# First feed-forward of a three-part transformer kernel: 512-column products of both operand parts, padded operand rows, and constants loaded later

## The reference, cut to what matters

```
h = rms_norm(x, g)
gate, val = split(h @ w_up)              # 2816 columns each
conv = conv_b + sum over 3 taps of shifted gate * conv_w
x = x + rms_norm((gelu(conv) * val) @ w_down, g_post)
```

## Time and profile before

| | us |
|---|---|
| median of three runs (lowest, highest) | 890.5 (890.3, 890.86) |
| the profiled execution, whole | 892.5 |
| its span, from the first to the last instruction | 890.5 |
| mean granted clock of PE over the span | 0.998 |

### The profile page before, as it was taken

How to read it: one execution, slowest core, us unless ns; L and a number is a source line. 1 busy time by engine, 2 the same in 40 slices (tenths; PEclk the granted TensorE clock), 3 DMA queues, 4 the chain that set the end, 5 groups by cost and what they waited for, 6 DMA issues and landing times.

```text
span 890.5 us, 17166 instructions
## 1 busy us (share of the span) xinstructions
PE 877.2 (99%) x6192; PEld 805.6 (90%) x6192; DVE 669.5 (75%) x1098; ACT 545.4 (61%) x859; POOL 71.0 (8%) x65
## 2 busy tenths in 40 slices
PE   9999999999999999999999999999999899999997
PEld 8977999999999999999999999999899898888886
DVE  6976887777777966879866676799787787667666
ACT  7265744344344755978866666677497777666663
POOL 1000000000000043000000040200120000003102
PEclk9999999999999999999999999999999999999999
DMA  8963275555655555435656556444334365655641
GB/s 319 336 229 106 96 242 181 190 184 173 207 170 187 165 190 188 144 119 168 202 179 206 189 170 201 150 143 142 127 117 146 116 216 184 204 183 179 202 147 48
DMA packets 44293, 156.85 MB, mean 176 GB/s; under 512 B 5098, under 2 KB 5589, under 8 KB 44117
## 3 DMA queue, kind: packets, MB, share of 16 engines
q1 hardware_dynamic: 42889, 152.32, 51.8%
q10 hardware_dynamic: 908, 2.28, 0.8%
q0 software_dynamic: 448, 1.59, 0.5%
HBM read 155.11 MB, written 1.06 MB: 175 GB/s over the span
## 4 chain that ended last, share of the span: by engine, by line
PE 87%; DVE 6%; ACT 2%; DMA 2%; issue 1%; ACTq 0%; POOL 0%; DVEq 0%; POOLq 0%
PE ps L431 13%; PE ps L432 13%; PE ps L433 13%; PE ps L664 13%; PE ps L666 7%; PE ps L503 5%; PE ps L505 5%; PE ps L504 5%; DMA w_gate<-in_w_gate 2%; DVE w_lo L1526 2%; PE ps L439 1%; PE ps L480 1%; PE ps L474 1%; PE ps L473 1%; PE ps L939 1%
## 5 line engine op out<-in xcount | busy, mean ns | idle before, releaser
L1526 DVE TENSOR_TENSOR w_lo<-raw,w_hi 128x1024 fp32r<-128x1024 f32 x222 | 273.3, 1257 | 25.9 <-ACT w_hi L1112 23.4
L1112 ACT ACTIVATE w_hi<-raw 128x1024 fp32r<-128x1024 f32 x223 | 226.7, 1051 | 40.4 <-PE ps L505 18.3
L431 PE MATMUL ps<-op_hi,w_hi 128*128 128x256 f32 (+1 forms) x794 | 225.1, 284 | 0.4 <-DVE op_lo L1713 0.4
L433 PE MATMUL ps<-op_hi,w_lo 128*128 128x256 f32 (+1 forms) x794 | 223.6, 282 | 0.0
L432 PE MATMUL ps<-op_lo,w_hi 128*128 128x256 f32 (+1 forms) x794 | 223.6, 282 | 0.0
L431 PEld LDWEIGHTS ps<-op_hi,w_hi 128*128 128x128 f32 x794 | 149.9, 189 | 3.2 <-issue 1.8
L432 PEld LDWEIGHTS ps<-op_lo,w_hi 128*128 128x128 f32 x794 | 149.9, 189 | 1.1
L433 PEld LDWEIGHTS ps<-op_hi,w_lo 128*128 128x128 f32 x794 | 149.7, 189 | 0.0
L664 PE MATMUL ps<-mix,w_hi 128*128 128x512 f32 x384 | 136.3, 392 | 0.0
L666 PE MATMUL ps<-mix,w_lo 128*128 128x256 f32 x384 | 107.4, 280 | 0.0
L431 PE MATMUL ps<-mix,w_hi 128*128 128x256 f32 x336 | 95.8, 285 | 0.2 <-DVE mix L1883 0.2
(11 more groups left out here) (332 smaller groups left out, 1391.3 us busy)
## 6 DMA issues: line engine op xcount, KB each, us to landing
raw<-in_stream SPq DMA_DIRECT2D x283, 512.0 KB, 3.7
bias<-bias_rows POOLq DMA_DIRECT2D x1, 1024.0 KB, 12.7
work<-in_last_norm SPq DMA_DIRECT2D x1, 1024.0 KB, 5.7
result<-y SPq DMA_DIRECT2D x4, 256.0 KB, 2.0
x<-in_x SPq DMA_DIRECT2D x3, 256.0 KB, 5.2
y<-in_spans ACTq DMA_DIRECT2D x1, 640.0 KB
raw<-in_stream SPq DMA_DIRECT2D x2, 256.0 KB, 3.2
bias<-bias_rows POOLq DMA_DIRECT2D x1, 512.0 KB, 15.7
```

The source lines that it names most:

```text
L431: pe.matmul(o, wh, xh, start=start, stop=False, **kw)
L433: return pe.matmul(o, wl, xh, start=False, stop=stop, **kw)
L1112: m = act.activation(w_hi[:, s, :], raw[:, s, :], ACT.Copy)
L1526: m = dve.tensor_tensor(w_lo[:, s, :], raw[:, s, :], fp(w_hi[:, s, :]), ALU.subtract)
```

## The change

The feed-forward of layer one takes the 512-column form from chunk 4 on, as a function `up_in_halves` for all three feed-forwards. For that, `op_hi` and `op_lo` become the two halves of one tensor, with rows of 272 elements (1088 bytes). ACT and DVE follow with `whole` from chunk 4: two copies by ACT and two additions by DVE more per chunk. Of the seven late constants, two (`wpool`, `p`) stay where they were; the other five are issued by POOL in the first feed-forward, after `h_ready` 6, and POOL converts `gmask` and `spans` there. `alpha_gain` and `alpha_shift` are made by POOL near the start, as soon as `vec` has landed. DVE waits for the last constants before the first windowed attention.

```diff
+OP_ROW = 272
-        op_hi_wide = sb("op_hi", [P, NCH, SEQ + 2], F32R)
-        op_lo_wide = sb("op_lo", [P, NCH, SEQ + 2], F32R)
+        op_both = sb("op", [P, 2, NCH, OP_ROW], F32R)
+        op_hi_wide, op_lo_wide = op_both[:, 0, :, 0:SEQ + 2], op_both[:, 1, :, 0:SEQ + 2]
...
-        late_consts = [("wpool", wpool[:]), ("masks", masks[:]), ("p", pt[:]), ("rope", rope[:]), ("gmask", gmask_f),
-                       ("spans", spans_f), ("w_gate", w_gate[:])]
+        late_consts = [("wpool", wpool[:]), ("p", pt[:])]
+        last_consts = [("masks", masks[:]), ("rope", rope[:]), ("gmask", gmask_f), ("spans", spans_f), ("w_gate", w_gate[:])]
...
-            pool.wait_ge(S["late_loaded"], 16 * len(late_consts))
-            pool.tensor_copy(gmask[:], gmask_f).then_inc(S["pool_const"], 1)
+            pool.wait_ge(S["vec_loaded"], 16)
+            own.done(pool.tensor_scalar(alpha_gain[:], vcol("ln_mix_g", 8, 8), ALPHA, None, ALU.mult))
+            own.settle()
+            pool.tensor_scalar(alpha_shift[:], vcol("ln_mix_b", 8, 8), ALPHA, None, ALU.mult).then_inc(S["alpha_made"], 1)
...
+            def load_last_consts(j):
+                chunk_passed(j)
+                for name, ap in last_consts:
+                    pool.dma_start(ap, d[name]).then_inc(S["last_consts_loaded"], 16)
+                pool.wait_ge(S["last_consts_loaded"], 16 * len(last_consts))
+                pool.tensor_copy(gmask[:], gmask_f).then_inc(S["pool_const"], 1)
+                pool.tensor_copy(spans[:], spans_f).then_inc(S["spans_rounded"], 1)
             row_roots(0)
             inverse_root(1)
+            load_last_consts(6)
             row_roots(1)
...
             inverse_root(6)
-            own.done(pool.tensor_scalar(alpha_gain[:], vcol("ln_mix_g", 8, 8), ALPHA, None, ALU.mult))
-            own.settle()
-            pool.tensor_scalar(alpha_shift[:], vcol("ln_mix_b", 8, 8), ALPHA, None, ALU.mult).then_inc(S["alpha_made"], 1)
             sum_normed_x(2 * NFF)
...
-                def up_normed(c):
+                def up_in_halves(c):
                     for b in (4 + 2 * c, 5 + 2 * c):
                         s = take()
                         for k in range(NCH):
-                            w, x_both = slice(k * P, k * P + P), normed(k)
+                            w = slice(k * P, k * P + P)
+                            x_both = normed(k) if shifted else op_both[:, :, k, 0:SEQ]
...
-                later = up
...
-                    later = up_normed
...
-                    later(0)
+                    up_in_halves(0)
...
-                        copy_half(conv[:, c, :], 5 + 2 * c, 0)
+                        copy_half((h_fp if convolve else conv)[:, c, :], 5 + 2 * c, 0)
...
-                    act.activation(spans[:], spans_f, ACT.Copy).then_inc(S["spans_rounded"], 1)
...
+                            if whole:
+                                dve.wait_ge(S["half_copied"], j * 2 + (halves0 + 1))
                             if convolve:
-                                chained(dve.tensor_tensor(g, chunk(up, 0), rinv[:, 0:SEQ], ALU.mult))
+                                if whole:
+                                    chained(dve.tensor_tensor(g, chunk(up, 0), g, ALU.add))
+                                chained(dve.tensor_tensor(g, g if whole else chunk(up, 0), rinv[:, 0:SEQ], ALU.mult))
...
                     elif whole:
                         dve.wait_ge(S["half_copied"], j * 2 + (halves0 + 2))
-                        chained(dve.tensor_tensor(conv[:, c, :], chunk(up + 1, 0), conv[:, c, :], ALU.add))
+                        u = (h_fp if convolve else conv)[:, c, :]
+                        chained(dve.tensor_tensor(u, chunk(up + 1, 0), u, ALU.add))
                         dve.wait_ge(S["gate_act"], j + (j0 + 1))
-                        chained(dve.tensor_tensor(h_fp[:, c, :], gate[:, c, :], conv[:, c, :], ALU.mult))
+                        chained(dve.tensor_tensor(h_fp[:, c, :], gate[:, c, :], u, ALU.mult))
...
+            dve.wait_ge(S["last_consts_loaded"], 16 * len(last_consts))
             pair_shift(4, over(masks[:, 1, :], 2), True)
```

More of the change, by code:

```diff
@@ L707, in feed_forward @@
                         pe.wait_ge(S["normed_lo"], 4 * norms[0])
-                    later(0)
+                    up_in_halves(0)
                     down(1, i * 2 + (j + 4 + done))
-                    later(1)
+                    up_in_halves(1)
                     unit.leave(turns)
                 down(0, j + NFF - 3)
-                later(0)
+                up_in_halves(0)
                 if shifted:
@@ L1298, in feed_forward @@
                     step()
-                    hidden_chunk(0, i * 2 + (4 + done), whole=not convolve)
+                    hidden_chunk(0, i * 2 + (4 + done), whole=True)
                     step()
-                    hidden_chunk(1, i * 2 + (5 + done), whole=not convolve)
+                    hidden_chunk(1, i * 2 + (5 + done), whole=True)
                     unit.leave(turns)
@@ L1305, in feed_forward @@
                 step()
-                hidden_chunk(0, NFF - 2, whole=not convolve)
+                hidden_chunk(0, NFF - 2, whole=True)
                 if mean:
@@ L1309, in feed_forward @@
                 step()
-                hidden_chunk(1, NFF - 1, whole=not convolve)
+                hidden_chunk(1, NFF - 1, whole=True)
                 step(ahead=not late)
@@ L1828, in feed_forward @@
                 j0 = hidden.n
-                halves0 = 2 * (NFF - 6) * normed_n[0] - 12
+                halves0 = -8 if convolve else 2 * (NFF - 4) + 2 * (NFF - 6) * normed_n[0] - 12
                 def wcol(at, j):
@@ L1868, in hidden_chunk @@
                     unit_done()
-                    if convolve:
+                    if convolve and not whole:
                         dve.wait_ge(S["gate_act"], j + (j0 + 1))
@@ L1902, in feed_forward @@
                     normed_n[0] += 1
-                turns, per = (NFF - done) // 2 - 3, 10 if convolve else 6
+                turns, per = (NFF - done) // 2 - 3, 14 if convolve else 6
                 with dve.Fori(0, turns) as i:
```

5 lines of the change are left out of this document (2 added, 3 removed).

## The result

The changed kernel takes 884.13 us (median of six runs, 883.58 to 884.38). The kernel before, in six runs beside it, takes 890.68 (890.13 to 892.9). The ratio is 0.9922, 95% interval 0.9909 to 0.9934: faster by 0.8%, where the forecast said 882.2. Timed once more on another chip the ratio was 0.9915 (0.9902 to 0.9928). The profiled execution of the changed kernel takes 883.58 us, with a span of 881.8: 8.7 us less span than the profiled execution before, against 6.55 us between the medians. These two differences are not the same number, and why is part of what follows.

The account below looks back on a forecast made before the run. PE, busy 99% of the span, was taken as the bound. Terms 3.0 + 4.0 + 1.5 - 0.25 = 8.25 us off 892.5 gave 884.25 profiled, 882.2 for the median; range 879.2 to 886.0, the forecast's own 881.0 to 883.2.

Parts of the forecast that it names:

- the early wait that stays: Rival, first mixer: PE's wait before the second scores remains, DVE held by PE's pool product or own order; 883.7, chance 0.12.
- the fixed part: Rival, first feed-forward: a product costs columns plus a fixed part, so fewer products save 0.7 for 3.0; 884.5, chance 0.05.
- 512-column products, 18 chunks: First feed-forward, chunks 4 to 21: period falls from 8.507 to the third feed-forward's 8.340, 3.0 us less.
- the last chunk: End of the first feed-forward: DVE is 1.52 later against a margin of 1.27, so PE waits 0.25 us; bounds 0, 0.6.
- `alpha` early: Head of the third feed-forward: PE's stall (2.59) and the slow clock behind it (1.42) go, 4.0 us; bounds 2.6, 4.2.
- loads out of the first mixer: First mixer: five loads fewer bring DVE 1.67 earlier, closing PE's wait before the scores, 1.5 us; bounds 0, 1.6.
- loads in their new place: First feed-forward: POOL's loads and two conversions may delay DVE 3.9 us once, within margin; price 0, up to 1.
- rows of 1088 bytes: Operand `op`: longer rows priced at 0; bound and rival, three-product units quicken by 2.4 us, 879.8, chance 0.10.
- the twin: The third feed-forward's loop, 12 chunks at 8.340 us each, taken as the same loop to price the 512-column form.
- DVE's slack: First feed-forward chunks: DVE works 7.99 in a period of 8.34, slack 0.35 us, so PE keeps the pace narrowly.
- The rival with DVE as the pace: First feed-forward: 0.3 to 0.5 more DVE work per chunk shrinks the 3.0 to about 0.3; 885.0, chance 0.14.
- the one that ends slower: Rival, first feed-forward: DVE needs more than 8.80 us per chunk, eating the other gains; at 9.0 the time is 894; chance 0.05.

## Why the prediction was right, and what was off

The time, 884.13, lies within the stated range (879.2 to 886.0), but not within the forecast's own (881.0 to 883.2). By itself it would fit two rivals as well, the early wait that stays (883.7) and the fixed part (884.5); the traces show that the wait went, and that the form gave three times the fixed part. By its own steps, the terms against the traces (before to after) and the runs:

| step | predicted | between the two traces | undone or alone |
|---|---|---|---|
| 512-column products, 18 chunks | 3.0 | 153.12 - 150.96 = 2.16 | 1.80 (trace), 0.9 to 1.9 (runs) |
| the last chunk | -0.25 | 5.61 - 5.93 = -0.32 | (trace) -0.34 |
| `alpha` early | 4.0 | 16.80 - 12.57 = 4.2 | 4.2 (trace), 3.15 (runs) |
| loads out of the first mixer | 1.5 | 59.40 - 57.70 = 1.70 | alone 1.64 (trace), 0.7 (runs); undone 0.55 (trace) |
| loads in their new place | 0 | 0 | 0 |
| rows of 1088 bytes | 0 | within the 2.16, and part of the rest | 1.42 (trace), 1.0 to 2.0 (runs) |
| not in the sum | | 8.7 - 7.7 = 1.0 | |

The rows of this table don't add up in the last column: form and rows each stand for the same gain, since neither brings much without the other.

*512-column products: the mechanism was right, the size was off.* 3.0 came from the twin's 8.340. What it missed is that the twin reads `mix`, with rows of 1024 bytes, where two up units take 5.55 us, and `op` gives 5.59 with rows of 1088 bytes. Of the rivals "a product costs its columns and a fixed part" came close to the form alone: 0.7 against 18 x (8.507 - 8.466) = 0.7 on rows of 1032 bytes. The forecast's objection, that the twin's rate holds on two tiles, was no evidence on `op`. By the rule of the Trainium skill that was set beside it ("TensorE: Matmul & The Clock Gate", "Back-to-back issue gap"), which that section gives for single, isolated products, it is the same 0.7; the traces agree on rows of 1032 bytes and give 1.8 on rows of 1088. They agree in the difference alone: by that rule a part of three products would take an estimated 0.33 us, and the traces have 2.85 / 8 = 0.36.

*Rows of 1088 bytes: this step failed.* It said "So 0", from gate units that take three products on rows of 1024 bytes. That is right for three products (5.70 with either row) and was carried to a form that it doesn't show. The bound of 2.4 us was near the right size for a wrong reason: luck. A second effect was not thought of at all: a longer tile moves the tiles behind it. The units of the gate stage, of which five served as evidence (2.85 each; six take 17.08 us from 296.04 on), took 2.80 each, 16.80 us for six, once `mix` had moved; but the kernels with early `alpha` alone and with the constants alone, where `mix` lies as before, have 16.90 there, so not all of that is its place. The 1.0 us that is not in the sum is made of such small pieces, many of them in stages on `mix`, and not all of one sign: the 12 chunks of the third feed-forward got 0.24 slower, 100.32 for 100.08.

*DVE's slack: right in kind.* 0.35 us was counted; most chunks of the loop have 0.51 to 0.55 idle (the mean of 0.59 holds 1.97 in the first chunk). One instruction of 0.45 fits, two don't. The additions cost less than the 1.10 that was counted, 206.88 - 206.43 = 0.45 for the gate's (its row above) and 202.39 - 201.85 = 0.54 for the value's:

```profile
201.85 0.42 DVE L1887 TENSOR_TENSOR proj<-ps,proj 128x256 f32<-128x256 f32 x1
202.39 0.43 DVE L1889 TENSOR_TENSOR proj<-proj 128x256 f32<-128x256 f32 x1
```

And the period is 0.05 longer than the forecast's. The rival with DVE as the pace, and the one that ends slower, needed 0.3 to 0.5 and 0.8 us more of DVE's work per chunk than was counted; it was less.

*The last chunk* came out at 0.32 for 0.25, and goes when its additions go.

*`alpha` made early:* 4.2 for 4.0 between the traces, and nothing took its place. *The early wait* went, 1.70 for 1.5, and 1.64 with the constants moved alone: its rival, that DVE is held by PE's pool product, shows up only as DVE's wait of 2.15 us, which leaves PE no wait before the scores.

*The sum held in part by luck.* 8.25 was forecast and the spans differ by 8.7, since the 0.84 us that the 512-column products fell short was made up by the 1.0 that no step had counted, and 0.4 more in `alpha` and the loads.

*From the profile to the median: the step that put the forecast 2 us too low.* It read "The profiled execution takes 892.5, so 884.25 profiled; the runs' median is 2.0 below it, so 882.2 for the median." The first half held: 883.58 profiled. The second took 2.0 us as a constant of profiling. It is not: the changed kernel's profiled execution (883.58) is no slower than its median (884.13). Nor was it well known: 890.5 was the median of three runs, and the 45 runs of the kernel before beside the experiments have 891.5, so about half of the 2.0 came with those three runs. The kernel with the constants alone shows what such 2 us can be: its runs stand in two groups 2 us apart, and the profiled one of the upper group has the lower clock behind PE's stand at the head of the third feed-forward. The execution profiled before had the same fall there, 1.42 us in the down unit alone. By this reading about 2.6 of `alpha`'s 4.2 us, the stand, is there in each execution, and the rest only in those where the clock falls. The 45 runs fit it: the 19 with a mean clock of 0.999 have a median of 890.8, the 13 with 0.997 or less one of 892.1. Where the median lies under the profiled execution, likely only a part of the runs pays it; the forecast counted it as gain in full and then subtracted the 2.0 as well. That each run's clock falls at this place was not shown.

## What to carry to other kernels

A term taken from a twin loop holds for the twin's operands: before it is borrowed, compare the tile, its rows and where it begins, and try form and layout together as well as apart. Check whether a stand of PE in the one profiled execution was followed by a fall of the clock; if it was, that part of the price may be paid in some runs only, and then belongs neither in full in the gain against the median nor in a constant offset. Slack of an engine beside the bound is tested by adding its work: a loop may hide an overdraft for ten turns and pay it at the end.

## What was not expected of the hardware

- Two up units in the 512-column form took 5.55 to 5.61 us on rows of 1024 bytes, by where the tile begins, 5.59 on 1088, 5.65 on 1088 with the parts side by side, 5.66 to 5.68 on 1032. Units in three products on `mix` took 2.80 to 2.88 us, most of it by where the tile begins. The Trainium skill, page "SBUF — State Buffer", section "Door 1: The DMA port swizzle", has SBUF read in lines of 16 bytes, with a penalty for each access that comes to a new line. Rows of 1032 bytes can't all begin at the start of such a line, and the 5.67 for 5.59 would fit; but three products on the same rows show no such difference (5.70 on 1032 and on 1088), and kernels whose tiles differ by multiples of 64 bytes still differ, 5.59 and 5.65, 2.80 and 2.88. So it explains little here, and what decides stays open.
- A stand of PE of 1.77 us was followed by the lower clock in one trace, and one of 1.58 at the same place in another trace was not. It cost 1.54 us more when it was (4.45 for 2.91). The two traces with the stand of 2.4 at the later place both show the lower clock behind it, for 1.4 and 1.6 us; that other runs keep the clock there is argued from their mean clock.
- POOL's conversions (1.04 and 1.44 us) stretched one DVE instruction each, by 0.38 and 0.66 us. Each of these had begun inside the conversion, and ended 0.28 and 0.15 us behind its end.
